# Experts' rows turned by a product with two stacked unit blocks, in a one-core block kernel

## The chip, the cores and the metric

The kernel runs on one core of a Trainium2 chip. The metric is the time of one execution on the device, in microseconds, as the median of several runs. The core has TensorE (PE in the profile's rows, its weight loads PEld), VectorE (DVE), ScalarE (ACT), GpSimd (POOL) and SyncE (SP), which issues most of the transfers.

## What is computed

Two transformer-like blocks on 256 tokens of width 1024, all in fp32. The change lies in the mixture of experts of the first block: each token goes to 2 of 32 experts, and each expert is a gated product with a hidden width of 256:

```python
def block_ffn(args):
    tok, wt, e = args
    xb = xt[tok]
    hb = jax.nn.silu(xb @ w_gate[e]) * (xb @ w_up[e])
    return (hb @ w_down[e]).astype(F32) * wt[:, None]
```

The rows are then added back to their tokens. Everything ahead of it (three mixers, router) and behind it (a gate, a convolution block, attention and two gated feed-forward layers) is untouched by the change.

## The kernel before, in words

The weights come as a stream of units of 128x2048 fp32 (1 MB each). For each unit a transfer fills one of 4 raw buffers, ScalarE rounds it to fp32r (`whi`, line 529, in halves line 538), VectorE takes the rest (`wlo = raw - whi`, line 1194, in halves 1205), and TensorE multiplies with both. `whi` and `wlo` are rings of 3 units: a unit may be rounded only when TensorE has used the unit three before it (`unit_used`). A raw buffer is filled again when VectorE has taken its rest (`low_done`).

The experts are done in 16 pairs, each with 6 units: two of gate and up for each expert, one of down for each. An expert has 64 slots. The order of the work is written out by hand, one queue for each engine (`pair_step` for TensorE, `pair_act` for ScalarE, `pair_dve` for VectorE); pairs 0, 1, 14 and 15 are unrolled, 2 to 13 run in a loop of four pairs a turn. In a pair:

- TensorE forms gate and up of the first expert in bank 0 (lines 2448 and 2449). The moving operand is the weights (512 columns), the stationary one the expert's tokens: 64 rows of rounded tokens and 64 rows of their rests, so that bank 0 has 128 rows, of which row s and row 64 + s must be added.
- It scatters the pair before (2500, 2501), gathers tokens for a later quad of experts (2431, 8 products here and 4 twice later; 16 in a pair), and turns the first expert's rows.
- ScalarE copies bank 0 to SBUF (`gu`, 754). `turn_rows` (2456) turns it in four blocks of 128 columns back into bank 0. `fold` on VectorE (1608) adds the turned rounded tokens' columns and rests' columns, 128x512 to 128x256, into `gut` in SBUF, and signals `summed`.
- ScalarE takes the Silu of the gate half (758), VectorE multiplies by the up half (`hidden`, 1613), ScalarE rounds it (762), VectorE takes the rest (`hidden_low`, 1617, signal `turned_ready`), and `pair_down` on TensorE multiplies with unit 4 (2042 to 2044).
- The second expert goes the same way in bank 1 and with unit 5. Between, `turn_slots` (2468, 2470) turns the choice of tokens for the scatter into bank 0; it waits for `summed` of the first expert, since it overwrites bank 0.

In the last two pairs (`x.last_quad`) nothing is gathered, and the order differs: VectorE takes unit 4 in halves with the sum between them, and ScalarE rounds unit 5 ahead of the first Silu.

Of the kernel before, what the change touches and what calls it, by code (L numbers as in the profile page):

```python
# [129 lines left out]
def program(nc, stream, table, params, finals, p_in, x_in, out):  # L130
    ctx = ExitStack()
    with ctx:
# [133 lines left out]
        gu = arena[:, 0:1024].rearrange("p (e n) -> p e n", e=2)  # L266
        gut = arena[:, 1024:1536].rearrange("p (e f s) -> p e f s", e=2, f=4)
        sgl = arena[:, 1536:1792].rearrange("p (e f s) -> p e f s", e=2, f=2)
# [224 lines left out]
        @block.sync  # L493
        def _(sp):
            for t in range(TT):
                sp.dma_start(xres[:, t, :], x_in[:, t, :]).then_inc(S(f"x{t}_loaded"), 16)
            for k in range(4):
                sp.dma_start(raw[:, 0, cols2(k)], stream[0][:, cols2(k)]).then_inc(S(f"piece{k}_landed"), 16)
            sp.dma_start(raw[:, 1, :], stream[1]).then_inc(S("landed1"), 16)
            sp.dma_start(cst[:, P:], table[:, P:]).then_inc(S("table_loaded"), 16)  # L500
            sp.dma_start(raw[:, 2, :], stream[2]).then_inc(S("landed2"), 16)
            sp.dma_start(par[:, GAINS:], params[:, GAINS:]).then_inc(S("params_loaded"), 16)
            sp.dma_start(raw[:, 3, :], stream[3]).then_inc(S("landed3"), 16)

            with sp.Fori(0, UNITS // RAW - 1) as j:
                for s in range(RAW):
                    sp.wait_ge(S("low_done"), RAW * j + s + 1)
                    sp.dma_start(raw[:, s, :], stream[RAW * j + (s + RAW)]).then_inc(S(f"landed{s}"), 16)
            for n, (t, c) in enumerate(((0, 0), (0, 1), (1, 0), (1, 1))):
                sp.wait_ge(*((S("y_ready"), 1), (S("y_ready"), 2), (S("y_half_ready"), 1), (S("y_ready"), 3))[n])  # L510
                sp.dma_start(out[:, t, cols2(c)], xn[:, t, cols2(c)]).then_inc(S("stored"), 16)
            sp.wait_ge(S("stored"), TT * 32)
# [3 lines left out]
        def _(act):  # L516
# [193 lines left out]
            split_to(16)  # L710
            act.dma_start(g2_row, finals[2]).then_inc(S("final_loaded"), 16)
            act.dma_start(p_t, p_in).then_inc(S("p_loaded"), 16)
            turn_y_act(2)
# [42 lines left out]
            def silu_pair(x, e):  # L756
                act.wait_ge(S("summed"), x.count(2, e + 1))
                act.activation(sgl[:, e], gut[:, e, 0:2, :], ACT.Silu).then_inc(S("pair_silu"), 1)

# [424 lines left out]
        def _(dve):  # L1184
# [419 lines left out]

            def fold(x, e):

                dve.wait_ge(S("rows_turned"), x.count(2, e + 1))
                dve.tensor_reduce(gut[:, e], bank[e][:].rearrange("p (f w s) -> p f s w", f=4, w=2), AX.X, ALU.add)\
                   .then_inc(S("summed"), 1)

            def hidden(x, e):
                dve.wait_ge(S("pair_silu"), x.count(2, e + 1))
                dve.tensor_tensor(hv[:, e], sgl[:, e], gut[:, e, 2:4, :], ALU.mult).then_inc(S("hidden_ready"), 1)

# [22 lines left out]
            def pair_dve(x):  # L1637
# [19 lines left out]
                if x.last_quad:  # L1657
                    split_part(x.unit(4), 0)
                    fold(x, 0)
                    split_part(x.unit(4), 1)  # L1660
                    hidden(x, 0)
                    hidden_low(x, 0)
                    fold(x, 1)
                    slot_weights(x)
                    hidden(x, 1)
                    split_part(x.unit(5), 0)
                    hidden_low(x, 1)
                    split_part(x.unit(5), 1)
                    return
                fold(x, 0)  # L1670
                ahead(4)
                hidden(x, 0)
                split_part(x.unit(5), 0)
                hidden_low(x, 0)
                fold(x, 1)
                slot_weights(x)
# [357 lines left out]
        def _(pe):  # L2034
# [418 lines left out]
            def turn_rows(x, e):  # L2453
                pe.wait_ge(S("gate_up_out"), x.count(2, e + 1))
                for f in range(4):
                    ins = pe.transpose(bank[e][:, P * f:P * f + P], gu[:, e, P * f:P * f + P], ident)  # L2456
                ins.then_inc(S("rows_turned"), 1)

            def turn_slots(x):

                pe.wait_ge(S("summed"), x.count(2, 1))
                if x.p0 == 0:
# [42 lines left out]
            def pair_step(x):  # L2505
# [4 lines left out]
                if x.p0:  # L2510
                    pe.wait_ge(S("summed"), x.count(2, -1))
                    pe.wait_ge(S("back_ready"), x.count(1))
# [4 lines left out]
                if x.last_quad:  # L2517

                    pe.wait_ge(S("summed"), x.count(2))
                    pair_gate_up(x, 1, (0,))  # L2520
# [12 lines left out]
                if x.p0:  # L2533
                    pe.wait_ge(S("summed"), x.count(2))
                pair_gate_up(x, 1)
# [36 lines left out]

            pe.wait_ge(S("summed"), 2 * PAIRS)
            pe.wait_ge(S("slot_weights"), PAIRS)
# [250 lines left out]
def constants():  # L2825

    t = np.zeros((P, CONST_W), np.float32)

# [19 lines left out]
    put("neghalf", np.full((P, 8), -0.5))  # L2848
    put("iota64", np.broadcast_to(1 + np.arange(SLOTS), (P, SLOTS)))
    return t  # L2850

# [108 lines left out]
```

## Time and profile before

| what | value |
|---|---|
| median of 3 runs | 1088.3 us (1086.83 to 1090.26) |
| the profiled execution | 1087.57 us |
| its span, first to last instruction | 1085.6 us |
| mean granted clock of TensorE | 0.996 |
| the experts' pairs | from 161 to 446 us of the span |
| VectorE's sum, 32 of them | 21.9 us busy |
| TensorE's turns of rows, 32 groups of 4 | 20.2 us busy |

The rows of the trace give start and length in microseconds. A matmul's length holds its way through the array, and matmuls overlap: what one costs is read from the distance between starts. Rows of VectorE overlap by some 0.08 us as well.

### The profile page before, as it was taken

What the parts mean: (1) busy time and instruction counts of PE and PEld (TensorE: products, weight loads), DVE (VectorE), ACT (ScalarE), POOL (GpSimd) and SP (SyncE); (2) the same over time, 40 slices, a digit from 0 to 9 for tenths busy, and PEclk for the clock granted to TensorE, in tenths of its full rate; (3) what the DMA queues carried; (4) which work ended last, traced back from release to release, by engine and by line L of the source; (5) the groups of instructions that cost most, each with busy time, mean ns of one, the idle gap of its engine ahead of it and who ended that gap; (6) DMA issues with size and microseconds to landing.
All of it is one profiled execution on the core that took longest, in us unless ns stands there. A gap on an engine that the chain in (4) does not pass through costs nothing.

```text
span 1085.6 us, 17366 instructions
## 1 busy us (share of the span) xinstructions
PE 1058.6 (98%) x6390; PEld 925.0 (85%) x6390; DVE 866.3 (80%) x1142; ACT 714.3 (66%) x962; POOL 144.1 (13%) x96
## 2 busy tenths in 40 slices
PE   7999989999999999999999999999999999999997
PEld 6877778888788887789989899998788889999986
DVE  5498689999999999877666777677777877876876
ACT  6676479898889898775435545445566766455553
POOL 3001100000000000012000334250200000432420
PEclk9999999999999999999999999999999999999999
DMA  9541528889988888754654454554433335545531
GB/s 369 189 155 39 206 82 347 348 346 333 346 331 337 343 344 334 285 209 156 225 180 178 155 213 161 206 193 155 173 137 118 116 120 211 207 156 217 184 126 40
DMA packets 33605, 232.64 MB, mean 214 GB/s; under 512 B 3856, under 2 KB 3984, under 8 KB 6032
## 3 DMA queue, kind: packets, MB, share of 16 engines
q1 hardware_dynamic: 32688, 229.98, 57.3%
q10 hardware_dynamic: 864, 1.93, 0.6%
q8 instruction: 35, 0.57, 0.2%
q14 instruction: 18, 0.15, 0.0%
HBM read 230.85 MB, written 1.05 MB: 214 GB/s over the span
## 4 chain that ended last, share of the span: by engine, by line
PE 78%; DVE 12%; ACT 5%; DMA 2%; issue 2%; POOL 0%; SPq 0%; DVEq 0%; ACTq 0%
PE bank L2042 11%; PE bank L2044 11%; PE bank L2043 11%; PE bank L2600 9%; PE bank L2601 8%; PE bank L2602 8%; DVE wlo L1194 4%; PE bank L2449 4%; PE bank L2448 4%; PE bank L2431 2%; ACT whi L529 2%; DMA raw<-stream 2%; DVE arena L1797 2%; PE bank L2456 1%; DVE wlo L1205 1%
## 5 line engine op out<-in xcount | busy, mean ns | idle before, releaser
L1194 DVE TENSOR_TENSOR wlo<-raw,whi 128x2048 fp32r<-128x2048 f32 x178 | 405.7, 2288 | 62.9 <-ACT whi L529 62.3
L529 ACT ACTIVATE whi<-raw 128x2048 fp32r<-128x2048 f32 x197 | 375.0, 1913 | 76.3 <-PE bank L2044 37.6
L2600 PE MATMUL bank<-xs,whi 128*128 128x256 f32 x896 | 251.2, 280 | 1.5 <-DVE wlo L1194 1.5
L2601 PE MATMUL bank<-xs,whi 128*128 128x256 f32 x896 | 250.2, 279 | 0.0
L2602 PE MATMUL bank<-xs,wlo 128*128 128x256 f32 x896 | 250.0, 279 | 0.0
L2600 PEld LDWEIGHTS bank<-xs,whi 128*128 128x128 f32 x896 | 168.4, 188 | 3.8 <-DVE wlo L1194 2.3
L2601 PEld LDWEIGHTS bank<-xs,whi 128*128 128x128 f32 x896 | 168.4, 188 | 0.9
L2602 PEld LDWEIGHTS bank<-xs,wlo 128*128 128x128 f32 x896 | 168.4, 188 | 0.0
L2042 PE MATMUL bank<-whi,rounded 128*128 128x512 f32 x344 | 138.4, 402 | 1.1 <-DVE wlo L1194 0.4
L2044 PE MATMUL bank<-whi,rounded 128*128 128x512 f32 x344 | 136.1, 396 | 0.0
L2043 PE MATMUL bank<-wlo,rounded 128*128 128x512 f32 x344 | 136.0, 395 | 0.0
L2042 PE MATMUL bank<-whi,xs 128*128 128x512 f32 (+1 forms) x304 | 121.0, 398 | 2.8 <-DVE xs L1312 0.9
L1155 POOL COPY cwn<-par 128x12 f32 (+1 forms) x22 | 93.3, 4247 | 199.5 <-DVE arena L1797 199.4
L2044 PE MATMUL bank<-whi,xs 128*128 128x512 f32 (+1 forms) x304 | 118.3, 389 | 0.0
L2043 PE MATMUL bank<-wlo,xs 128*128 128x512 f32 (+1 forms) x304 | 118.2, 389 | 0.0
L1797 DVE SCALAR_TENSOR_TENSOR arena<-arena,cwn 128x255 f32<-128x255 f32 (+1 forms) x160 | 66.7, 480 | 34.6 <-ACT arena L846 33.9
L846 ACT ACTIVATE arena<-arena,cwn 128x256 f32<-128x256 f32 x80 | 34.2, 499 | 86.2 <-DVE arena L1786 86.2
L1087 POOL TENSOR_SCALAR total<-sumsq 128x1 f32<-128x1 f32 x14 | 7.2, 512 | 628.7 <-ACT xn L563 628.2
L1205 DVE TENSOR_TENSOR wlo<-raw,whi 128x1024 fp32r<-128x1024 f32 x66 | 79.2, 1220 | 1.9 <-ACT whi L529 1.7
L2042 PEld LDWEIGHTS bank<-whi,rounded 128*128 128x128 f32 x344 | 64.6, 188 | 18.1 <-issue 3.6
L2044 PEld LDWEIGHTS bank<-whi,rounded 128*128 128x128 f32 x344 | 64.6, 188 | 15.6
L2043 PEld LDWEIGHTS bank<-wlo,rounded 128*128 128x128 f32 x344 | 64.7, 188 | 13.1
(342 smaller groups left out, 1655.2 us busy)
## 6 DMA issues: line engine op xcount, KB each, us to landing
raw<-stream SPq DMA_DIRECT2D x215, 1024.0 KB, 4.9
arena<-finals ACTq DMA_DIRECT2D x3, 512.0 KB, 5.6
xres<-x_in SPq DMA_DIRECT2D x2, 512.0 KB, 4.8
raw<-stream SPq DMA_DIRECT2D x4, 256.0 KB, 6.1
out<-xn SPq DMA_DIRECT2D x4, 256.0 KB, 2.1
par<-params SPq DMA_DIRECT2D x1, 844.0 KB, 12.4
cst<-table SPq DMA_DIRECT2D x1, 502.0 KB, 8.8
arena<-p_in ACTq DMA_DIRECT2D x1, 256.0 KB, 5.9
```

Of the source, the lines that this page charges most:

```text
L529: act.activation(whi[:, s, :], raw[:, a, :], ACT.Copy).then_inc(S("high_done"), 1)
L1155: pool.tensor_copy(cwn[:, b, :], src).then_inc(S("taps_ready"), 1)
L1194: dve.tensor_tensor(wlo[:, s, :], raw[:, unit0 % RAW, :], whi[:, s, :].bitcast(F32), ALU.subtract)\
L1205: ins = dve.tensor_tensor(wlo[:, s, w], raw[:, unit0 % RAW, w], whi[:, s, w].bitcast(F32), ALU.subtract)
L1797: ins = dve.scalar_tensor_tensor(a, fraw[:, b, f, 0:T - 2 + k], cwn[:, b, 4 * k + f:4 * k + f + 1], a, ALU.mult, ALU.add)
L2042: pe.matmul(o, ah, bh, start=start, stop=False, skip_group_check=True)
L2043: pe.matmul(o, ah, bl, start=False, stop=False, skip_group_check=True)
L2044: return pe.matmul(o, al, bh, start=False, stop=stop, skip_group_check=True)
L2448: pe.matmul(bank[e][:], tokens, whi[:, s, c], start=kk == 0, stop=False, skip_group_check=True)
L2600: pe.matmul(o, whi[:, s, w], xhi[:, kk, :], start=first, stop=False, skip_group_check=True)
L2601: pe.matmul(o, whi[:, s, w], xlo[:, kk, :], start=False, stop=False, skip_group_check=True)
L2602: ins = pe.matmul(o, wlo[:, s, w], xhi[:, kk, :], start=False, stop=kk == 7, skip_group_check=True)
```

## The change

`turn_rows` no longer turns `gu` with the unit matrix. It multiplies each block of 128 columns, as the stationary operand, by `stack`, a matrix of 128x64 with two unit blocks of 64 on each other, in plain fp32. The product has, for each of the block's 128 columns, 64 values: row s plus row 64 + s. It lies in 256 columns of the bank. VectorE's sum is left out; the Silu and the hidden product read the bank itself. The waits on `summed` become waits on `hidden_ready`. `stack` is a new part of the constants' table, fetched by one more transfer on ScalarE's queue.

```diff
--- before.py
+++ after.py
@@ -264,7 +264,9 @@
               for a in (arena_r[:, 6144:10240], xs[:].rearrange("p w k t -> p (w k t)"))]
 
         gu = arena[:, 0:1024].rearrange("p (e n) -> p e n", e=2)
-        gut = arena[:, 1024:1536].rearrange("p (e f s) -> p e f s", e=2, f=4)
+        gut = [bank[e][:, 0:256].rearrange("p (f s) -> p f s", f=4) for e in range(2)]
+
+        stack = arena[:, 10240:10240 + SLOTS]
         sgl = arena[:, 1536:1792].rearrange("p (e f s) -> p e f s", e=2, f=2)
         hv = arena[:, 1792:2048].rearrange("p (e f s) -> p e f s", e=2, f=2)
         xg2 = arena[:, 6144:6144 + TT * D].rearrange("p (a n) -> p a n", a=TT)
@@ -497,7 +499,7 @@
             for k in range(4):
                 sp.dma_start(raw[:, 0, cols2(k)], stream[0][:, cols2(k)]).then_inc(S(f"piece{k}_landed"), 16)
             sp.dma_start(raw[:, 1, :], stream[1]).then_inc(S("landed1"), 16)
-            sp.dma_start(cst[:, P:], table[:, P:]).then_inc(S("table_loaded"), 16)
+            sp.dma_start(cst[:, P:], table[:, P:CONST_W]).then_inc(S("table_loaded"), 16)
             sp.dma_start(raw[:, 2, :], stream[2]).then_inc(S("landed2"), 16)
             sp.dma_start(par[:, GAINS:], params[:, GAINS:]).then_inc(S("params_loaded"), 16)
             sp.dma_start(raw[:, 3, :], stream[3]).then_inc(S("landed3"), 16)
@@ -709,6 +711,7 @@
             turn_y_act(1)
             split_to(16)
             act.dma_start(g2_row, finals[2]).then_inc(S("final_loaded"), 16)
+            act.dma_start(stack, table[:, CONST_W:]).then_inc(S("table_loaded"), 16)
             act.dma_start(p_t, p_in).then_inc(S("p_loaded"), 16)
             turn_y_act(2)
             def tokens_high(t):
@@ -754,8 +757,8 @@
                 act.activation(gu[:, e, :], bank[e][:], ACT.Copy).then_inc(S("gate_up_out"), 1)
 
             def silu_pair(x, e):
-                act.wait_ge(S("summed"), x.count(2, e + 1))
-                act.activation(sgl[:, e], gut[:, e, 0:2, :], ACT.Silu).then_inc(S("pair_silu"), 1)
+                act.wait_ge(S("rows_turned"), x.count(2, e + 1))
+                act.activation(sgl[:, e], gut[e][:, 0:2, :], ACT.Silu).then_inc(S("pair_silu"), 1)
 
             def hidden_high(x, e):
                 act.wait_ge(S("hidden_ready"), x.count(2, e + 1))
@@ -1602,15 +1605,9 @@
             pick_quad(slice(4, 8), 1, S("pick_ready"))
             split_to(U_MOE + 3)
 
-            def fold(x, e):
-
-                dve.wait_ge(S("rows_turned"), x.count(2, e + 1))
-                dve.tensor_reduce(gut[:, e], bank[e][:].rearrange("p (f w s) -> p f s w", f=4, w=2), AX.X, ALU.add)\
-                   .then_inc(S("summed"), 1)
-
             def hidden(x, e):
                 dve.wait_ge(S("pair_silu"), x.count(2, e + 1))
-                dve.tensor_tensor(hv[:, e], sgl[:, e], gut[:, e, 2:4, :], ALU.mult).then_inc(S("hidden_ready"), 1)
+                dve.tensor_tensor(hv[:, e], sgl[:, e], gut[e][:, 2:4, :], ALU.mult).then_inc(S("hidden_ready"), 1)
 
             def hidden_low(x, e):
                 dve.wait_ge(S("turned_high"), x.count(2, e + 1))
@@ -1656,23 +1653,19 @@
 
                 if x.last_quad:
                     split_part(x.unit(4), 0)
-                    fold(x, 0)
+                    hidden(x, 0)
                     split_part(x.unit(4), 1)
-                    hidden(x, 0)
                     hidden_low(x, 0)
-                    fold(x, 1)
                     slot_weights(x)
                     hidden(x, 1)
                     split_part(x.unit(5), 0)
                     hidden_low(x, 1)
                     split_part(x.unit(5), 1)
                     return
-                fold(x, 0)
                 ahead(4)
                 hidden(x, 0)
                 split_part(x.unit(5), 0)
                 hidden_low(x, 0)
-                fold(x, 1)
                 slot_weights(x)
                 hidden(x, 1)
                 split_part(x.unit(5), 1)
@@ -2452,13 +2445,17 @@
 
             def turn_rows(x, e):
                 pe.wait_ge(S("gate_up_out"), x.count(2, e + 1))
+
+                if x.p0 == 0 and e == 0:
+                    pe.wait_ge(S("table_loaded"), 32)
                 for f in range(4):
-                    ins = pe.transpose(bank[e][:, P * f:P * f + P], gu[:, e, P * f:P * f + P], ident)
+                    ins = pe.matmul(bank[e][:, SLOTS * f:SLOTS * f + SLOTS], gu[:, e, P * f:P * f + P], stack, start=True,
+                                    stop=True, skip_group_check=True)
                 ins.then_inc(S("rows_turned"), 1)
 
             def turn_slots(x):
 
-                pe.wait_ge(S("summed"), x.count(2, 1))
+                pe.wait_ge(S("hidden_ready"), x.count(2, 1))
                 if x.p0 == 0:
                     pe.wait_ge(S("wt_ready"), 3)
                 pe.wait_ge(S("pick_ready"), x.quads(1))
@@ -2508,7 +2505,7 @@
                         pe.wait_ge(S("gather_out"), x.count(4, 5 + m))
                     gather(1 - x.buf, 4 * x.second + m, 2 + m % 2)
                 if x.p0:
-                    pe.wait_ge(S("summed"), x.count(2, -1))
+                    pe.wait_ge(S("hidden_ready"), x.count(2, -1))
                     pe.wait_ge(S("back_ready"), x.count(1))
                     pe.wait_ge(S("slot_weights"), x.count(1))
                 pair_gate_up(x, 0)
@@ -2516,7 +2513,7 @@
                     scatter(x.count(1))
                 if x.last_quad:
 
-                    pe.wait_ge(S("summed"), x.count(2))
+                    pe.wait_ge(S("hidden_ready"), x.count(2))
                     pair_gate_up(x, 1, (0,))
                     turn_rows(x, 0)
                     pair_gate_up(x, 1, (1,))
@@ -2531,7 +2528,7 @@
                 fetch(1)
                 turn_rows(x, 0)
                 if x.p0:
-                    pe.wait_ge(S("summed"), x.count(2))
+                    pe.wait_ge(S("hidden_ready"), x.count(2))
                 pair_gate_up(x, 1)
                 fetch(2)
                 turn_slots(x)
@@ -2570,7 +2567,7 @@
                 if tiles[-1] == TT - 1:
                     ins.then_inc(S("unit_used") if c else S("projected"), 1)
 
-            pe.wait_ge(S("summed"), 2 * PAIRS)
+            pe.wait_ge(S("hidden_ready"), 2 * PAIRS)
             pe.wait_ge(S("slot_weights"), PAIRS)
             overflow_pe(pe)
             pe.wait_ge(S("wt_ready"), 4)
@@ -2824,7 +2821,7 @@
 
 def constants():
 
-    t = np.zeros((P, CONST_W), np.float32)
+    t = np.zeros((P, CONST_W + SLOTS), np.float32)
 
     def put(name, v):
         a, b = CONST[name]
@@ -2847,6 +2844,7 @@
     put("iota32", np.broadcast_to(np.arange(NE) - 64.0, (P, NE)))
     put("neghalf", np.full((P, 8), -0.5))
     put("iota64", np.broadcast_to(1 + np.arange(SLOTS), (P, SLOTS)))
+    t[:, CONST_W:] = i % SLOTS == np.arange(SLOTS)[None, :]
     return t
```

On VectorE, a pair's part from the low part of unit 4 on (pair 1, the unrolled one): L1608 is the sum, L1194 and L1205 the units' rests, L1613 the hidden product, L1617 its rest, L1634 the slots' weights. Before:

```order
L1194 TENSOR_TENSOR wlo<-raw,whi 128x2048 [waits high_done] x2
L1608 TENSOR_REDUCE arena<-bank 128x256 [waits rows_turned]
L1194 TENSOR_TENSOR wlo<-raw,whi 128x2048 [waits high_done]
L1613 TENSOR_TENSOR arena<-arena 128x128 [waits pair_silu]
L1205 TENSOR_TENSOR wlo<-raw,whi 128x1024 [waits high_done]
L1617 TENSOR_TENSOR rounded<-arena,rounded 128x2x64 [waits turned_high]
L1608 TENSOR_REDUCE arena<-bank 128x256 [waits rows_turned]
L1634 TENSOR_REDUCE sm<-bank 64x1 [waits back_ready]
L1634 TENSOR_REDUCE sm<-bank 64x1
L1613 TENSOR_TENSOR arena<-arena 128x128 [waits pair_silu]
L1205 TENSOR_TENSOR wlo<-raw,whi 128x1024
```

and with the change, where these lines are 1197, 1208, 1610, 1614 and 1631:

```order
L1197 TENSOR_TENSOR wlo<-raw,whi 128x2048 [waits high_done] x3
L1610 TENSOR_TENSOR arena<-arena,bank 128x128 [waits pair_silu]
L1208 TENSOR_TENSOR wlo<-raw,whi 128x1024 [waits high_done]
L1614 TENSOR_TENSOR rounded<-arena,rounded 128x2x64 [waits turned_high]
L1631 TENSOR_REDUCE sm<-bank 64x1 [waits back_ready]
L1631 TENSOR_REDUCE sm<-bank 64x1
L1610 TENSOR_TENSOR arena<-arena,bank 128x128 [waits pair_silu]
L1208 TENSOR_TENSOR wlo<-raw,whi 128x1024
L1614 TENSOR_TENSOR rounded<-arena,rounded 128x2x64 [waits turned_high]
```

Both sums are gone. The hidden product reads the bank beside `arena`, and nothing stands between the rests of units 3 and 4.

On TensorE, the turning of slots in pair 0 and the second expert's rows behind it, before:

```order
L2468 MATMUL bank<-cst,rounded 128x128 [waits pick_ready,wt_ready,summed]
L2468 MATMUL bank<-cst,rounded 128x128
L2470 MATMUL bank<-rounded 128x4 x2
L2456 MATMUL bank<-cst,arena 128x128 [waits gate_up_out]
L2456 MATMUL bank<-cst,arena 128x128 x3
```

and with the change:

```order
L2465 MATMUL bank<-cst,rounded 128x128 [waits pick_ready,wt_ready,hidden_ready]
L2465 MATMUL bank<-cst,rounded 128x128
L2467 MATMUL bank<-rounded 128x4 x2
L2452 MATMUL bank<-arena 128x64 [waits gate_up_out]
L2452 MATMUL bank<-arena 128x64 x3
```

The order is the same. The slots' first instruction waits for the hidden product instead of the sum, and the turn has become a product of 64 columns.

On VectorE in pair 15, one of the last two, from unit 4's first half on, before:

```order
L1205 TENSOR_TENSOR wlo<-raw,whi 128x1024 [waits high_done]
L1608 TENSOR_REDUCE arena<-bank 128x256 [waits rows_turned]
L1205 TENSOR_TENSOR wlo<-raw,whi 128x1024
L1613 TENSOR_TENSOR arena<-arena 128x128 [waits pair_silu]
L1617 TENSOR_TENSOR rounded<-arena,rounded 128x2x64 [waits turned_high]
L1608 TENSOR_REDUCE arena<-bank 128x256 [waits rows_turned]
L1634 TENSOR_REDUCE sm<-bank 64x1 [waits back_ready]
L1634 TENSOR_REDUCE sm<-bank 64x1
L1613 TENSOR_TENSOR arena<-arena 128x128 [waits pair_silu]
```

and with the change:

```order
L1208 TENSOR_TENSOR wlo<-raw,whi 128x1024 [waits high_done]
L1610 TENSOR_TENSOR arena<-arena,bank 128x128 [waits pair_silu]
L1208 TENSOR_TENSOR wlo<-raw,whi 128x1024
L1614 TENSOR_TENSOR rounded<-arena,rounded 128x2x64 [waits turned_high]
L1631 TENSOR_REDUCE sm<-bank 64x1 [waits back_ready]
L1631 TENSOR_REDUCE sm<-bank 64x1
L1610 TENSOR_TENSOR arena<-arena,bank 128x128 [waits pair_silu]
```

The hidden product, which waits for ScalarE's Silu, stands where the sum stood, ahead of unit 4's second half; before it stood behind it.

## Rows read from the trace of the kernel before

**Rows 1.** the page, busy us (share of the span) xinstructions of each engine

```profile
PE 1058.6 (98%) x6390; PEld 925.0 (85%) x6390; DVE 866.3 (80%) x1142; ACT 714.3 (66%) x962; POOL 144.1 (13%) x96
```

**Rows 2.** window, length, PE, PEld, DVE, ACT, POOL busy (x), PEclk, DMA, GB/s

```profile
220.00:240.00 20.00, 20.00 (x106) 16.81 (x105) 19.25 (x24) 18.19 (x24) 0.00 (x0) 1.00 0.89 341
```

**Rows 3.** waits of the stage: us in total, times, longest

```profile
ACT whi L529 <- DMA raw<-stream: 5.1, 8, 1.2
...
ACT arena L758 <- DVE arena L1608: 4.3, 7, 1.0
...
PEld bank L2042 <- issue: 2.8, 12, 0.3
```

**Rows 4.** TensorE from pair 4 to pair 6: start, length, line, operation, [idle <-releaser]

```profile
234.73 0.60 PE L2456 MATMUL bank<-cst,arena 128*128 128x128 f32 x4
235.09 0.48 PE L2448 MATMUL bank<-whi,arena_r 128*128 128x512 f32 x1
235.41 0.41 PE L2449 MATMUL bank<-wlo,arena_r 128*128 128x512 f32 x1
235.65 0.39 PE L2448 MATMUL bank<-whi,arena_r 128*128 128x512 f32 x1
...
238.92 0.64 PE L2431 MATMUL bank<-rounded,arena_r 128*128 128x256 f32 x4
239.40 0.38 PE L2468 MATMUL bank<-cst,rounded 128*128 128x128 f32 x2
...
240.19 0.72 PE L2431 MATMUL bank<-rounded,arena_r 128*128 128x256 f32 x4
241.02 0.50 PE L2042 MATMUL bank<-whi,rounded 128*128 128x512 f32 x1
...
276.21 0.38 PE L2468 MATMUL bank<-cst,rounded 128*128 128x128 f32 x2
```

**Rows 5.** VectorE in order of time, pair 4

```profile
236.37 0.68 DVE L1608 TENSOR_REDUCE arena<-bank 128x256 f32<-128x512 f32 x1
236.97 2.28 DVE L1194 TENSOR_TENSOR wlo<-raw,whi 128x2048 fp32r<-128x2048 f32 x1
239.17 0.28 DVE L1613 TENSOR_TENSOR arena<-arena 128x128 f32<-128x128 f32 x1
239.37 1.22 DVE L1205 TENSOR_TENSOR wlo<-raw,whi 128x1024 fp32r<-128x1024 f32 x1
240.51 0.29 DVE L1617 TENSOR_TENSOR rounded<-arena,rounded 128x128 fp32r<-128x128 f32 x1
```

**Rows 6.** VectorE and TensorE in order of time, pair 5

```profile
257.70 1.23 DVE L1205 TENSOR_TENSOR wlo<-raw,whi 128x1024 fp32r<-128x1024 f32 x1 [0.19 <-ACT whi L529]
258.85 0.28 DVE L1617 TENSOR_TENSOR rounded<-arena,rounded 128x128 fp32r<-128x128 f32 x1
...
259.36 0.49 PE L2042 MATMUL bank<-whi,rounded 128*128 128x512 f32 x1
```

**Rows 7.** TensorE in order of time, plain fp32 products of 64 columns

```profile
100.21 1.90 PE L2249 MATMUL bank<-arena,par 128*128 128x64 f32 x16
101.94 0.65 PE L2239 MATMUL bank<-mixer 96*128 96x256 f32 x2
...
113.66 0.33 PE L2281 MATMUL bank<-arena 128*128 128x64 f32 x2
113.83 0.39 PE L2282 MATMUL bank<-arena 128*128 128x64 f32 x2
```

**Rows 8.** ScalarE in order of time, pair 4, unit 5 rounded

```profile
237.31 1.90 ACT L529 ACTIVATE whi<-raw 128x2048 fp32r<-128x2048 f32 x1
```

**Rows 9.** ScalarE, VectorE and TensorE in order of time, pair 14

```profile
423.96 0.29 ACT L758 ACTIVATE arena<-arena 128x128 f32<-128x128 f32 x1
...
423.40 1.22 DVE L1205 TENSOR_TENSOR wlo<-raw,whi 128x1024 fp32r<-128x1024 f32 x1
...
431.74 0.48 PE L2448 MATMUL bank<-whi,xs 128*128 128x512 f32 x1 [0.33 <-DVE wlo L1205]
```

## The prediction

> **What bounds the kernel now.** The change sits in the experts' stage alone, the stretch from 161 to 446 us, so I read the page's busy shares first and then left them. TensorE is busy 98% of the span and VectorE 80% [rows 1]; over the whole span nothing says which of the two the experts wait for. A window inside the stage says more: TensorE busy 20.00 of 20 us, VectorE 19.25, ScalarE 18.19, the DMA engines 0.89 [rows 2]. All four are nearly full, so the question is which wait ends last in TensorE's own stream, not who is busy.
>
> The waits of the stage name few for TensorE: 2.8 us put down to "issue" ahead of the first product of the down projection, 12 times. The sum that the change removes (L1608) is waited for 4.3 us, 7 times, but by ScalarE [rows 3].
>
> Then the stream of one pair of experts. Pair 4's and pair 6's slots are turned at 239.40 and 276.21 us [rows 4]: two pairs take 36.81 us, one 18.40. TensorE's own work in a pair: 64 products of 512 columns (32 gate and up, 24 down, 8 scatter) that start 0.235 us apart (235.41 to 235.65), 15.0 us; 16 gathers 0.12 apart (238.92 to 239.40 for four), 1.9; two groups of four turns, 0.45 and 0.50 with the slower start behind them, and the slots 0.37. That is 18.2 of 18.40 us. What is left, 0.2 to 0.3 us, I look for where a start is late. The last gathers of pair 4 start at 240.19, so the next product is due at 240.67; it starts at 241.02 [rows 4]. What it needs is the rest of the first expert's hidden rows, VectorE's L1617, which ends at 240.80 [rows 5]. This 0.35 us is the "issue" of the waits. In pair 5 the same rest ends at 259.13 and the product starts at 259.36 [rows 6]; by the same release time of 0.2 us it is 0.19 late there. **The stage is bound by TensorE's stream plus this one late operand per pair.**
>
> **The change, part by part.**
>
> 1. Turning with a sum. 32 groups of four turns (128 columns) become 32 groups of four products of 64 columns in full fp32. The turns: the group begins at 234.73, the next product at 235.09, and the one behind it only at 235.41, where 0.235 is usual [rows 4]: 0.36 + 0.32 - 0.235 = 0.45 us for the group. The nearest row for the new kind is the same shape, plain fp32, 64 columns, 16 in a row: from 100.21 to the next product at 101.94, so 0.108 us apart [rows 7]. Four are 0.43, and with the same 0.09 for the slower first fp32r product behind them 0.52. Where plain fp32 products follow fp32r ones, the first pair starts together in 0.17 instead of 0.22 us [rows 7], which gives 0.48. I take +0.03 for the first expert's group and nothing for the second's, which stands between small products on both sides: **16 x 0.03 = +0.5 us**, with ends -0.6 (0.02 less in each) and +2.2 (0.07 more in each).
>
> A rule speaks against this step. The Trainium skill, "TensorE: Matmul & The Clock Gate", section Terms, says that transpose mode is four times faster for FP32, and "FP8 and Floating Point Precision", section TensorE Precision Notes, that true FP32 takes four passes. By them 64 columns of product would cost as much as 256 of a turn, twice what a turn of 128 costs. The rows disagree: turn and product both start 0.11 apart; the sum by the rule is the third rival below.
>
> 2. The sum on VectorE, 0.68 us each (L1608 at 236.37, the next row starts 0.60 later) [rows 5], goes 32 times. TensorE never waits for it directly. What it holds up:
> - First expert. In pair 4 (and in the even pairs 2 to 12) VectorE is busy without a gap through the sum, the low part of unit 4 (L1194), the hidden product (L1613), half of unit 5 (L1205) and the rest (L1617) [rows 5]. Without the sum everything up to L1613 comes 0.60 earlier. But L1205 needs ScalarE's high part of unit 5, which runs from 237.31 to 239.21 and in pair 5 is itself held by TensorE's use of the ring (VectorE waits 0.19 us for ScalarE there) [rows 6, 8]. ScalarE's wait for the sum ahead of its Silu, 0.6 us on average [rows 3], goes too, but the same ring holds unit 5 until about 237.25. So L1205 starts near 239.25 instead of 239.37, and the late operand comes 0.12 us earlier: **6 even pairs x 0.12 = -0.7 us**. Odd pairs gain nothing. Ends: 0 and, if the whole wait went in all 16 pairs, -16 x 0.27 = -4.3 us (the mean of 0.35 and 0.19).
> - Second expert. Its Silu waits in ScalarE's queue behind the last gather's copy, not behind the sum. 0, covered by that queue.
> - VectorE's 0.60 x 2 becomes idle time. What is late next is ScalarE's unit 5.
>
> 3. Silu and the hidden product read the bank instead of SBUF. The sum itself read 512 columns of a bank in 0.68 us [rows 5], so 128 cannot cost much over the 0.28 of the hidden product now. 0, covered by VectorE's new idle time; without that cover some 0.05 us a pair (an estimate from those two rows).
>
> 4. A new, later wait. Turning the slots writes bank 0, where the turned rows now stay until the hidden product has read them. So TensorE waits for L1613 in place of the sum. Behind it in TensorE's queue stand the slots, the second expert's turn, the last gather and the down projection, and behind those ScalarE's copy of the slots and its last rounding. Before, L1613 of pair 4 ends at 239.45, 0.05 us *after* the slots start at 239.40 [rows 4, 5]: at the old times the wait would bite in every even pair. With the sum gone it ends near 238.85, 0.55 ahead, and in pair 5, where L1194 is ready as early, it is better still. 0 in the loop.
>
> 5. The last two pairs. There ScalarE rounds unit 5 ahead of the first Silu, and VectorE now stands in L1613 with half of unit 4 behind it. Pair 14: ScalarE's Silu runs from 423.96 to 424.25, and VectorE's second half of unit 4, now from 423.40 to 424.62 [rows 9], comes behind the hidden product: 424.25 + 0.28 + 1.22 = 425.7. The rest of the hidden rows, which TensorE's down projection needs, comes behind that, some 0.45 us later than now. But VectorE then has 1.2 us less to do up to 431.6, where TensorE waits 0.33 us for it [rows 9]. Pair 15 is alike. I take **-0.1 us for both**, ends -1.0 and +1.0.
>
> 6. One more transfer of 32 KB on ScalarE's DMA queue, behind the one for p, and a first wait for it. 0: it is asked for before the experts' routing begins and is first used behind the first pair's gate and up.
>
> Sum: +0.5 - 0.7 - 0.1 = **-0.3 us**. The profiled execution took 1087.6 us (span 1085.6 and 2.0 around it), 0.7 under the median of 1088.3; against the median the change gives 1088.0.
>
> **The rivals.**
>
> *VectorE was the bound (faster).* It is busy 19.25 of 20 us, and if all that TensorE waits for in a pair hangs on VectorE's load, 0.2 to 0.3 us per pair go and the last pairs' micro-waits with them: -4.3 - 1 + 0.5, about 1083.5. Against it: TensorE's stream fills 18.2 of 18.40, and the operand is held by ScalarE's unit 5, not by the sum. A softer form is that VectorE's slack lets transfers be asked for earlier and saves a late DMA or two (5.1 us of ScalarE's waits are for them [rows 3]), 1 to 2 us. Chance 0.17 of over 3.3 us.
>
> *The new wait bites (slower).* Place: turning the slots in each pair. It decides where L1613 ends later than about 0.1 us ahead of the slots, that is if less than 0.15 of the 0.60 us comes through in even pairs. Then TensorE, which has no slack, loses 0.05 plus 0.2 for the release in each of 16 pairs, 4 us, and the last two pairs 0.9 with nothing given back: 1088.0 + 5 = 1093. For: the order of the queues before is exactly at that edge. Against: wlo of unit 4 has its high part ready long before (ScalarE does it ahead of the gathers' copies). Chance 0.11.
>
> *The product costs twice a turn (slower).* If a turn's spacing of 0.11 us hid part of its price, and a plain product added 0.054 more, TensorE would lose 128 x 0.054 = 6.9 us: 1095. The rule of the Trainium skill's page "TensorE: Matmul & The Clock Gate", section Terms, would make it so. The 16 products 0.108 apart speak against it. Chance 0.07.
>
> *Nothing measurable.* My forecast is this case: both edits move less than a measurement can tell, which for this kernel I put at 0.3%, 3.3 us. Chance 0.65.
>
> **How the numbers follow.** Likeliest 1088.0. Range 1084.0 to 1091.5: down to the faster rival's neighbourhood, up by the +2.2 and +1.0 ends; what it leaves out is the two slower rivals and the far end of the faster one, under 0.2. Faster by over 0.3% 0.17, within 0.65, slower 0.18 (0.11 + 0.07).
>
> **What would show it.** Products of 64 columns starting 0.11 us apart, the 32 groups taking 14 to 16 us in all. VectorE busy 20 us less, in a window like that of the busy shares near 18 of 20 us with TensorE still at 20.00. The down projection's late start in even pairs 0.35 down to about 0.2, unchanged in odd ones. No wait of TensorE at the slots in pairs 1 to 13, one of some 0.6 us in pairs 14 and 15. A period of a pair under 18.2 or over 18.6 us would make the forecast wrong.

## The result: slower by 0.77%

The change took 1095.35 us in the median (1095.04 to 1096.25, 4 runs), the kernel before 1087.57 (1085.91 to 1090.26, 4 runs, the three from ahead of the prediction among them): a ratio of 1.0077, with a 95% interval from 1.0064 to 1.009, and 7.8 us more between the medians (the ratio is estimated from all the runs and is not the quotient of the medians, here and below). The profiled execution took 1095.46 us, its span 1093.7, 8.1 over that of before.

### The profile after

The page's busy times of the change, answering to [rows 1]:

```profile
PE 1069.8 (98%) x6518; PEld 938.4 (86%) x6518; DVE 846.9 (77%) x1110; ACT 711.7 (65%) x962; POOL 143.7 (13%) x96
```

TensorE holds 11.2 us more, in 128 more matmuls (6518 for 6390); VectorE holds 19.4 us less, in 32 fewer instructions. The sum is gone as planned, and something has been *added* on TensorE that the program doesn't list: it issues as many products as it issued turns. The window of [rows 2]:

```profile
core 0: us, PE busy (x) PEld busy (x) DVE busy (x) ACT busy (x) POOL busy (x), PEclk, DMA share, GB/s
220.00:240.00 20.00, 20.00 (x105) 16.85 (x105) 17.43 (x20) 16.65 (x22) 0.00 (x0) 1.00 0.87 329
```

VectorE fell from 19.25 to 17.43 us of 20; TensorE stayed at 20.00. The waits from 160 to 455 us (in total, times, longest):

```profile
DVE arena L1610 <- ACT arena L761: 21.1, 18, 2.1
DVE wlo L1208 <- ACT whi L531: 15.1, 14, 1.3
ACT whi L531 <- PE bank L2442: 13.7, 15, 1.1
...
PEld bank L2035 <- DVE rounded L1614: 2.2, 14, 0.2
ACT whi L531 <- DMA raw<-stream: 1.5, 1, 1.5
```

VectorE now waits, for Silu and for unit 5's rounding, and ScalarE waits 13.7 us for TensorE to free the ring. Transfers hold ScalarE once, 1.5 us, where it was 8 times and 5.1 us in the same window before [rows 3]. TensorE's own waits are small. So nothing that was relieved is what TensorE stands on; its stream has become longer. In order of time, pair 4 and pair 6's slots, as in [rows 4]:

```profile
start us, us, engine line op out<-in xcount [idle before <-releaser]
237.31 1.00 PE L2452 MATMUL bank<-arena 128*128 128x64 f32 x8
238.12 0.49 PE L2441 MATMUL bank<-whi,arena_r 128*128 128x512 f32 x1
238.44 0.40 PE L2442 MATMUL bank<-wlo,arena_r 128*128 128x512 f32 x1
...
241.95 0.64 PE L2424 MATMUL bank<-rounded,arena_r 128*128 128x256 f32 x4
242.44 0.38 PE L2465 MATMUL bank<-cst,rounded 128*128 128x128 f32 x2
...
242.80 1.10 PE L2452 MATMUL bank<-arena 128*128 128x64 f32 x8
243.72 0.72 PE L2424 MATMUL bank<-rounded,arena_r 128*128 128x256 f32 x4
244.28 0.40 PE L2035 MATMUL bank<-whi,rounded 128*128 128x512 f32 x1
...
280.62 0.38 PE L2465 MATMUL bank<-cst,rounded 128*128 128x128 f32 x2
```

Pair 4's and pair 6's slots are 38.18 us apart, so a pair takes 19.09 us (its period) where it took 18.40, over the 18.6 that the prediction named as the sign of its being wrong. The first group of four products is recorded as **x8**, from 237.31 to the next product at 238.12 and the one behind it at 238.44: 0.81 + 0.32 - 0.235 = 0.90 us for the group, by the same reckoning that gave 0.45 for four turns. The second group, from 242.80 to 243.72, takes 0.92. The down projection's first product starts at 244.28, and is no longer late: due at 243.72 + 0.48 = 244.20, and 0.08 is what it shows in the pairs with no wait at all. All matmuls of the line, and the same view of two lines of before:

```profile
L2452 PEld LDWEIGHTS bank<-arena x256: 186/192/192, 160.9 to 452.2; 128*128 128x128 f32 x128
L2452 PE MATMUL bank<-arena x256: 217/275/323, 160.9 to 452.2; 128*128 128x64 f32 x128
```

```profile
L2249 PE MATMUL bank<-arena,par x16: 222/275/275, 100.2 to 101.8; 128*128 128x64 f32 x16
...
L2456 PE MATMUL bank<-cst,arena x128: 270/273/329, 161.1 to 443.4; 128*128 128x128 f32 x128
```

Line 2452 has 256 records and 256 weight loads; the program issues 128 products there. In the kernel before line 2249 has 16 records, and its loops (`for t in range(TT): for g in range(SGG)`) issue 8. The turns' 128 are 128. **A plain fp32 product is two recorded matmuls (called passes below), each with a weight load of its own, about 0.11 us apart at this width; a turn in transposing mode is one.** I had read 0.108 us between *records* as 0.108 us a *product*.

### The profile page after: what moved, and what is told of

The parts are those of the page before. It is cut to its first block, busy times and chain, and to the rows that moved or that the text cites. A ratio compares the mean times of both kernels' runs of the same rounds, so it can differ in the third digit from the quotient of the medians.

```text
span 1093.7 us, 17592 instructions
## 1 busy us (share of the span) xinstructions
PE 1069.8 (98%) x6518; PEld 938.4 (86%) x6518; DVE 846.9 (77%) x1110; ACT 711.7 (65%) x962; POOL 143.7 (13%) x96
## 4 chain that ended last, share of the span: by engine, by line
PE 84%; DVE 10%; ACT 3%; issue 1%; DMA 1%; POOL 0%; SPq 0%; DVEq 0%; ACTq 0%
PE bank L2035 11%; PE bank L2037 11%; PE bank L2036 11%; PE bank L2597 9%; PE bank L2598 8%; PE bank L2599 8%; PE bank L2441 5%; PE bank L2442 5%; DVE wlo L1197 3%; PE bank L2424 3%; PE bank L2452 3%; DVE arena L1790 2%; PE bank L2498 1%; PE bank L2497 1%; ACT whi L531 1%
## 5 line engine op out<-in xcount | busy, mean ns | idle before, releaser
L1208 DVE TENSOR_TENSOR wlo<-raw,whi 128x1024 fp32r<-128x1024 f32 x66 | 79.2, 1220 | 15.2 <-ACT whi L531 15.1
```

Of the source, the lines that this page charges most:

```text
L1208: ins = dve.tensor_tensor(wlo[:, s, w], raw[:, unit0 % RAW, w], whi[:, s, w].bitcast(F32), ALU.subtract)
```

## The experiments

Each median stands beside runs of the kernel before that were taken with it on the same chip. The sum kept or not, and turn or product, make four kernels, of which two are the kernel before and the change; e2 and e4 are the other two.

### e1: every product twice

```diff
-                for f in range(4):
+                for f in 2 * list(range(4)):
                     ins = pe.matmul(bank[e][:, SLOTS * f:SLOTS * f + SLOTS], gu[:, e, P * f:P * f + P], stack, start=True,
```

> The change, with each of the 128 products of 64 columns issued twice (the same output written again). Theory A (a plain fp32 product is two passes of 0.11 us, 0.22 together, where a turn is one): 128 more products cost 128 x 0.22 = 28 us on a TensorE without slack, 1095.4 + 28 = 1123 us. Rival B (a product costs 0.11 like a turn, and the change lost its time in the new waits): +14 us, 1109.

Measured: 1125.19 us (before 1087.48, ratio 1.0351, 1.033 to 1.0371). That is 29.8 us over the change, 0.23 for each of 128 products. The line's records, 512 for 256 products:

```profile
L2452 PE MATMUL bank<-arena x512: 217/275/323, 161.8 to 481.2; 128*128 128x64 f32 x171
```

Theory A holds, 2 us over its 1123 us; rival B's 14 us is out by a factor of two.

### e2: the turns of before, the change's waits, no sum

```diff
-        gut = [bank[e][:, 0:256].rearrange("p (f s) -> p f s", f=4) for e in range(2)]
+        gut = [bank[e][:].rearrange("p (f w s) -> p f w s", f=4, w=2)[:, :, 0] for e in range(2)]
...
-                    ins = pe.matmul(bank[e][:, SLOTS * f:SLOTS * f + SLOTS], gu[:, e, P * f:P * f + P], stack, start=True,
-                                    stop=True, skip_group_check=True)
+                    ins = pe.transpose(bank[e][:, P * f:P * f + P], gu[:, e, P * f:P * f + P], ident)
```

> The change with its waits and without VectorE's sum, but with the four turns of before in place of the products; Silu and hidden product read only the rounded tokens' half of the bank, so the rests' half is left out of the result. Theory A: TensorE's stream is as before, and only the part of the late operand that hung on VectorE is gained: 1085.5 to 1087.5 us. Rival B (the waits are what cost): about 1095, as the change.

Measured: 1085.86 us (10 runs, before 1087.48 in 13), ratio 0.9985, 0.9973 to 0.9997. All that taking VectorE's sum away can bring, with the later wait paid, is some 1.6 us (0.3 to 2.9 by the interval). Rival B's 1095 is out: these waits are not what cost. TensorE in pair 4 (slots, second group of turns, last gathers, first product of the down projection) and pair 6's slots:

```profile
238.90 0.38 PE L2464 MATMUL bank<-cst,rounded 128*128 128x128 f32 x2
...
239.27 0.66 PE L2452 MATMUL bank<-cst,arena 128*128 128x128 f32 x4
239.69 0.72 PE L2424 MATMUL bank<-rounded,arena_r 128*128 128x256 f32 x4
240.36 0.49 PE L2035 MATMUL bank<-whi,rounded 128*128 128x512 f32 x1
...
275.55 0.38 PE L2464 MATMUL bank<-cst,rounded 128*128 128x128 f32 x2
```

A pair takes 36.65 / 2 = 18.33 us. The product due at 239.69 + 0.48 = 240.17 starts at 240.36, 0.19 late for 0.35 before: 0.16 gained in this even pair, where I forecast 0.12. The odd pairs show 0.19 too, as before. VectorE in the same pair:

```profile
237.93 0.28 DVE L1610 TENSOR_TENSOR arena<-arena,bank 128x128 f32<-128x128 f32 x1
238.71 1.23 DVE L1208 TENSOR_TENSOR wlo<-raw,whi 128x1024 fp32r<-128x1024 f32 x1 [0.49 <-ACT whi L531]
239.85 0.29 DVE L1614 TENSOR_TENSOR rounded<-arena,rounded 128x128 fp32r<-128x128 f32 x1
```

The hidden product ends at 238.21, well ahead of the slots at 238.90, so the new wait costs nothing in the loop (in pairs 14 and 15 the slots wait 0.68 and 0.24 us in this trace); L1208 waits 0.49 us for ScalarE's unit 5. Both are as the prediction had them.

### e3: the kernel before, with every turn made twice

```diff
-                for f in range(4):
+                for f in 2 * list(range(4)):
                     ins = pe.transpose(bank[e][:, P * f:P * f + P], gu[:, e, P * f:P * f + P], ident)
```

> The kernel before with each group of four turns issued twice: 32 x 4 x 0.11 = 14 us more of TensorE's time at the same places as the products', with VectorE's sum kept. If TensorE's slack ahead of the down projection (0.2 to 0.35 us a pair) takes up part of it whatever VectorE does: 1087.6 + 14.1 - 4.3 = 1097 us. If only VectorE's relief can give time back: 1101 to 1102.

Measured: 1096.52 us (ratio 1.0086, 1.0069 to 1.0103), 9.0 us over before, near the 1097 expected if TensorE's slack takes up part of any longer stream. The slots of pairs 4 and 6, with pair 4's second group and last gathers between:

```profile
243.32 0.38 PE L2468 MATMUL bank<-cst,rounded 128*128 128x128 f32 x2
...
243.70 1.09 PE L2456 MATMUL bank<-cst,arena 128*128 128x128 f32 x8
244.54 0.72 PE L2431 MATMUL bank<-rounded,arena_r 128*128 128x256 f32 x4
...
281.35 0.38 PE L2468 MATMUL bank<-cst,rounded 128*128 128x128 f32 x2
```

A pair takes 38.03 / 2 = 19.02 us, 0.62 more, though the stream got 8 turns longer, some 0.84 us (244.54 - 243.70 = 0.84 for its second group of eight, against 239.69 - 239.27 = 0.42 for four in e2, so 0.42 more for each of the two groups). The missing 0.2 is the late operand: the second group stands between what releases unit 5 and the product that needs the hidden rows' rest, so every 0.4 us put there hides up to 0.4 us of that wait. In this trace the down projection starts on time, within 0.08 us, in the loop's pairs.

### e4: the products, with the sum kept

```diff
-                    ins = pe.transpose(bank[e][:, P * f:P * f + P], gu[:, e, P * f:P * f + P], ident)
+                    ins = pe.matmul(bank[e][:, P * f:P * f + SLOTS], gu[:, e, P * f:P * f + P], stack, start=True,
+                                    stop=True, skip_group_check=True)
```

with `stack` fetched as in the change, and all else as before. It leaves the true sum out: half of the columns that VectorE adds are stale, and only its time counts.

> The products of the change, but VectorE's sum and the waits of before kept (the sum reads 64 new and 64 stale columns of each block, so it stands for its time alone). Theory A with the slack taken up by any longer stream of TensorE: 1095 to 1096 us, the same as the change, since the sum is hidden. Rival C (the change would cost 13.4 us and VectorE's relief gives 5.6 of them back): 1101.

Measured: 1097.68 us (ratio 1.0102, 1.0085 to 1.0119), 10.2 us over before. The slots of pairs 4 and 6:

```profile
242.71 0.38 PE L2473 MATMUL bank<-cst,rounded 128*128 128x128 f32 x2
...
281.00 0.38 PE L2473 MATMUL bank<-cst,rounded 128*128 128x128 f32 x2
```

The period is 38.29 / 2 = 19.15 us. The four kernels in one table (medians; the change was timed beside other runs of the kernel before, and 7.8 is its difference to those):

| over the kernel before, us | sum kept | sum gone |
|---|---|---|
| turns | 0 | -1.6 (e2) |
| products | +10.2 (e4) | +7.8 (the change) |

The products cost 9.4 to 10.2 us, and the sum's going gives 1.6 to 2.4. Of the 14 us that 128 more passes come to, the rest is taken up by the late operand and, as far as single traces tell, by transfers that no longer come late, in e3 and e4 too, with the sum still there. Neither my theory that the sum is hidden altogether (1095 to 1096) nor rival C (1101) hit e4, and the truth lies between them, nearer the first.

### e5: the later wait alone

```diff
             def turn_slots(x):
-                pe.wait_ge(S("summed"), x.count(2, 1))
+                pe.wait_ge(S("hidden_ready"), x.count(2, 1))
```

> The kernel before with one wait changed: turning the slots waits for the first expert's hidden product instead of the sum. At VectorE's old load the hidden product ends 0.05 us after the slots' start in the even pairs. If the forecast's edge is real: about 0.25 us in each of 8 even pairs and 0.3 in the last two, +2 to +3 us, 1090. If the late operand behind it takes it up: within 0.5 us of before. Rival B needs most of 7.8 us here.

Measured: 1087.21 us (10 runs, before 1086.31 in 13), ratio 1.0009, 0.9999 to 1.0018: 0.9 us, which its interval does not quite tell from nothing, and which lies between the two expectations. The waits from 160 to 450 us, and the late operand's in the same window of the kernel before:

```profile
PEld bank L2468 <- DVE arena L1613: 3.0, 4, 1.2
...
PEld bank L2042 <- issue: 2.2, 10, 0.8
PE bank L2468 <- DVE arena L1613: 1.7, 3, 0.8
```

```profile
PEld bank L2042 <- issue: 3.6, 13, 0.8
```

TensorE does stand at the slots, 3.0 us of weight loads in all. Part of that comes off the next wait: the late operand's "issue" is 2.2 us for 3.6 before. By these rows, a wait put ahead of another on the same engine is partly paid out of it; it is one trace, and the total is too small to say more.

### e6: the change, with VectorE's order of before in the last two pairs

```diff
                     split_part(x.unit(4), 0)
-                    hidden(x, 0)
                     split_part(x.unit(4), 1)
+                    hidden(x, 0)
                     hidden_low(x, 0)
```

> The change, with VectorE's order of before in the last two pairs: unit 4's second half ahead of the hidden product. The forecast put the price of this order at -0.1 for both pairs between -1 and +1: within 1 us of the change, 1094.4 to 1095.4. If the last pairs carry a part of the loss, it is 1 us or more faster.

Measured: 1095.84 us (ratio 1.0083, 1.0066 to 1.01); the change had 1.0077. It is 0.4 us above the expected range, and no difference to the change that these runs show. From pair 14's slots to the end of the span are 1094.3 - 433.01 = 661.3 us here and 1093.7 - 432.14 = 661.6 in the change.

### e7: the product in fp32r

```diff
-        gu = arena[:, 0:1024].rearrange("p (e n) -> p e n", e=2)
+        gu = arena_r[:, 0:1024].rearrange("p (e n) -> p e n", e=2)
+        stack_r = arena_r[:, 1024:1024 + SLOTS]
...
-                    ins = pe.matmul(bank[e][:, SLOTS * f:SLOTS * f + SLOTS], gu[:, e, P * f:P * f + P], stack, start=True,
+                    ins = pe.matmul(bank[e][:, SLOTS * f:SLOTS * f + SLOTS], gu[:, e, P * f:P * f + P], stack_r, start=True,
```

and ScalarE makes `stack_r` from `stack` once, ahead of the pairs.

> The change with gate and up rounded once more on ScalarE's copy out of the bank, so that the product with the two unit blocks is in fp32r instead of plain fp32; what it leaves out is the part of gate and up below fp32r's precision. Theory A (plain fp32 is two passes, fp32r one): one record of 64 columns per product, 0.11 us apart as the turns', the pair's period back from 19.09 to about 18.34 us, 1085.5 to 1086.5 us in all, as the kernel with turns and no sum, and under the kernel before. If the product's price has another cause than its passes: 1095.

Measured: 1084.93 us (11 runs, one of them 1092.01; before 1086.35 in 15), ratio 0.9995, 0.998 to 1.001. That is 0.6 under the expected range, and far from the 1095 of another cause. The line's records, one for each product, and the slots of pairs 4 and 6:

```profile
L2455 PE MATMUL bank<-arena_r x128: 193/277/299, 161.3 to 440.3; 128*128 128x64 f32 x128
```

```profile
239.19 0.38 PE L2468 MATMUL bank<-cst,rounded 128*128 128x128 f32 x2
...
275.86 0.38 PE L2468 MATMUL bank<-cst,rounded 128*128 128x128 f32 x2
```

The period is 36.67 / 2 = 18.34 us. The same 128 products of the same shape, rounded, take half the passes, and 0.75 us a pair goes. This and e1 settle the cause.

### e8: turns of 128 columns as plain fp32 products

```diff
-                    ins = pe.transpose(bank[e][:, P * f:P * f + P], gu[:, e, P * f:P * f + P], ident)
+                    ins = pe.matmul(bank[e][:, P * f:P * f + P], gu[:, e, P * f:P * f + P], ident, start=True, stop=True,
+                                    skip_group_check=True)
```

> The kernel before, with its turns of 128 columns made as plain fp32 products with the unit matrix instead of in the transposing mode; sum and waits kept. If each of the two passes costs 0.11 us whatever the columns (64 or 128), the price is that of the products of 64 columns with the sum kept: 1097 to 1098 us. If a pass goes by its columns in this range, 128 columns cost up to twice as much, 32 x 0.9 us more on top: 1110 us or more.

Measured: 1097.44 us (ratio 1.0096, 1.0079 to 1.0113), that of e4 with 64 columns. The line's records, and pair 4's first group:

```profile
L2456 PE MATMUL bank<-cst,arena x256: 270/275/377, 161.1 to 453.7; 128*128 128x128 f32 x128
```

```profile
237.81 1.05 PE L2456 MATMUL bank<-cst,arena 128*128 128x128 f32 x8
238.62 0.48 PE L2448 MATMUL bank<-whi,arena_r 128*128 128x512 f32 x1
```

128 columns are two passes of 0.10 us (237.81 to 238.62 for eight), as 64 are. So halving the columns from 128 to 64 bought nothing: in this range the price does not go by the columns. Whether it is the weight load that sets it, no run here shows.

Above 128 columns it does go by them. The kernel before has wider plain fp32 products ahead of the experts, each again in two records:

```profile
98.03 0.81 PE L2212 MATMUL bank<-arena,cst 128*128 128x384 f32 x2
98.68 0.38 PE L2213 MATMUL bank<-arena,cst 128*128 128x128 f32 x2
98.90 0.60 PE L2239 MATMUL bank<-mixer 96*128 96x256 f32 x2
99.33 0.38 PE L2240 MATMUL bank<-mixer 96*128 96x128 f32 x2
```

From start to start, a product of 384 columns takes 0.65 us, one of 128 columns 0.22 and one of 256 columns 0.43. An fp32r product of 256 columns takes 0.12 (four gathers from 238.92 to 239.40 [rows 4]). So plain fp32 costs 3.6 times fp32r at 256 columns, and the factor of two measured in this case belongs to narrow products.

### e9 and e10: the rounded product once more

e9 is e7 with e6's order; e10 is e7 unchanged, for a narrower interval.

> The product in fp32r on once more rounded rows (gate and up lose what lies below fp32r's precision), and in the last two pairs VectorE's order of before. Between pairs 14 and 15 the order of before gave 18.0 us for 18.9 with the plain product; here the stream has 0.45 us less in each group, so I expect no more than 0.5 us less than without the reordering, 1084.4 to 1085.5 us, and a ratio to before of 0.998 to 0.999.

> The rounded product in fp32r again, unchanged, since its first interval (0.998 to 1.001) holds no difference while its median is 1.4 us under that of before. If it is a gain, the ratio is 0.998 to 0.999 with an interval under 1; if the first median was chance, an interval around 1.

Measured: e9 1084.08 us (ratio 0.9981, 0.9969 to 0.9992; 0.3 under the expected range), e10 1084.85 (0.9984, 0.9975 to 0.9993), before 1086.88 in 20 runs. Both are faster than the kernel before, by 2.8 and 2.0 us in the medians, and some 10 us faster than the change; the order makes no difference between them that these runs show. The 0.9 us between pairs 14 and 15 that the expectation of e9 names was no gain in itself: e6 and the change take the same time from pair 14's slots on, within 0.3 us. It is bought with precision: e7, e9 and e10 round gate and up once more, where the kernel before carried them in full fp32.

## Why the prediction was wrong

**The forecast, the range and two of the rivals missed.** 1088.0 and 1084.0 to 1091.5 against 1095.35. The rival that hit, to the microsecond (1095), is "the product costs twice a turn", to which I gave 0.07. It had the cause, and the number by luck: its sum added 0.054 us a product, half of what its name says, 6.9 us in all, and gave nothing back. Measured, a product adds 0.11 us, 14.4 in all, and some 6 of them come back elsewhere.

- *Step 1, the price of a product: wrong, and all of the miss.* I took "16 in a row, 0.108 us apart" for sixteen products. They were eight products in sixteen records. The sum should have had, for a group, 4 x 0.216 + 0.09 less 0.05 = 0.90 against 0.45, so 32 x 0.45 = +14.4 us instead of +0.5. Even my upper end, +2.2, was built on the same misreading, so the range could not catch it. The evidence was in [rows 7] itself, beside the loops of the program: x16 for 8 issued. I also weighed the rule of the Trainium skill the wrong way round. The Trainium skill's page "FP8 and Floating Point Precision", section TensorE Precision Notes, has true FP32 at four passes; the trace records two for a product. In time the Trainium skill's four is nearer than the records' two once the product is wide: at 256 columns a plain product takes 3.6 times an fp32r one (e8), and only the narrow ones here take about twice. The Trainium skill's page "TensorE: Matmul & The Clock Gate", section Terms, has transposing four times faster for FP32; here the ratio is two with 64 columns (0.90 to 0.45 us a group), as the prediction worked it out from that rule, but it is two with 128 columns as well (e8), where the rule would make it four. The direction was right, and I set it aside for a row that I had not counted.
- *Step 2, the sum's going: right.* -0.7 us forecast in the loop, and between the traces of before and of e2 the late operand gains 0.15 to 0.18 us in five of the six even pairs, 0.07 in pair 6, 0.9 in all; 1.6 us was measured for the whole. VectorE was not the bound: the faster rival (1083.5) needed 4.8 us. In e2 transfers also come late less often (period 18.33 with 0.77 us lost in two pairs, for 1.6 us lost in pairs 6 and 7 before), which I read from single traces and haven't isolated.
- *The odd pairs and the late operand: half right.* I had it unchanged at 0.19 us in odd pairs. With a stream longer by 0.45 us behind unit 5's release it is gone in all pairs. Over the 0.08 that is there without a wait, it was 0.27 us in pair 4 and 0.11 in pair 5, and 2.3 us in pairs 2 to 13 together; pair 1 had none.

The rest of the way from 14.4 to 8.1 us is a reckoning from two traces and not tested by a run. It is in the slots' rows of the kernel before for pairs 7, 8 and 15 (pair 6 is in [rows 4]):

```profile
295.45 0.38 PE L2468 MATMUL bank<-cst,rounded 128*128 128x128 f32 x2
...
314.63 0.38 PE L2468 MATMUL bank<-cst,rounded 128*128 128x128 f32 x2
...
441.82 0.38 PE L2468 MATMUL bank<-cst,rounded 128*128 128x128 f32 x2
...
442.98 0.66 PE L2456 MATMUL bank<-cst,arena 128*128 128x128 f32 x4 [0.66 <-ACT arena L754]
```

From pair 6 to 7 and from 7 to 8 it takes 19.24 and 19.18 us for the usual 18.4, with transfers that came late; the change has 19.1 there as everywhere. That is 1.6 us, and it belongs to the one trace: e5, whose stream is as long, shows no such wait for a transfer. From pair 15's slots to the end of the span are 643.8 us before and 642.7 now, 1.1 less, although one more group lies there (0.45), so 1.6 came back at the end of the stage. Not all of that is relief: before, TensorE waits 0.66 us behind these slots, and in the change 0.71 ahead of them. With the sum kept the stretch is 644.0 us (e3) and 644.2 (e4). In the pairs between, 3.0 us came back: the 2.3 of the late operand and 0.7 or more that I can't place. 14.4 - 1.6 - 1.6 - 3.0 = 8.2.

- *Step 4, the new wait in the loop: right for the change* (VectorE's L1610 ends at 241.29, the slots start at 242.44). My price for its biting, 4 us and more, was too high: e5, where it does bite, cost 0.9.
- *Step 5, the last two pairs: no measurable effect,* as forecast (e6). The wait at the slots is there in pair 15, 0.71 us; in pair 14 TensorE waits 0.34 at the second group instead:

```profile
432.99 0.77 PE L2452 MATMUL bank<-arena 128*128 128x64 f32 x5 [0.34 <-ACT arena L757]
...
451.01 0.44 PE L2465 MATMUL bank<-cst,rounded 128*128 128x128 f32 x2 [0.71 <-DVE arena L1610]
```

- *Steps 3 and 6: nothing seen.* Silu from the bank takes 0.30 us where it took 0.31, the hidden product 0.28 as before.

VectorE's rows of pair 4, which carry steps 2 and 4:

```profile
241.01 0.28 DVE L1610 TENSOR_TENSOR arena<-arena,bank 128x128 f32<-128x128 f32 x1
242.23 1.23 DVE L1208 TENSOR_TENSOR wlo<-raw,whi 128x1024 fp32r<-128x1024 f32 x1 [0.95 <-ACT whi L531]
243.38 0.29 DVE L1614 TENSOR_TENSOR rounded<-arena,rounded 128x128 fp32r<-128x128 f32 x1
```

L1208 waits 0.95 us for ScalarE, which itself waits for TensorE. The relief landed where there was nothing to relieve.

## What to carry to other kernels

Before a duration per record is used as a price per instruction, count the records against the instructions that the program issues; a TensorE without slack pays for hidden passes, in full in e1, and in the change less what they hid of its own waits. Moving work from an engine with a few per cent of room to the one with none pays only if it costs the full one less than the waits it removes, and here the whole prize, taken alone, was 1.6 us. In such a place it also pays to ask in which precision the added product must be: rounded, the same product fits the old stream (e7). A wait of the full engine can swallow a part of any time added just ahead of it, whichever edit adds it.

## What the runs showed of the hardware

- A plain fp32 product of 64 columns is recorded as two weight loads and two matmuls, some 0.11 us apart, 0.23 us a product in e1; the same shape in fp32r is one (e7), and a transposing turn of fp32 is one.
- Between 64 and 128 columns the price of a plain fp32 product does not move (e4 1097.68, e8 1097.44 us); at 128, 256 and 384 columns it is 0.22, 0.43 and 0.65 us.
- The runs of the kernel before scatter over 4.8 us (1085.43 to 1090.26, all of them), the four of the change over 1.2 (1095.04 to 1096.25), and those of e1, e3, e4, e6 and e8, whose streams are longer too, over 1.6 at most in each. That the transfers have room there is a guess: ScalarE waits for one once in the change's trace and 8 times in that of before, but never in the experts' stage of e5.
